# Third block of a hybrid decoder trunk: head outputs with tokens on partitions, and where the norm factor is applied

## The reference

```python
def _head_norm(o, g, center):
    if center:
        o = o - jnp.mean(o, axis=-1, keepdims=True)
    o = o * lax.rsqrt(jnp.mean(jnp.square(o), axis=-1, keepdims=True) + EPS)
    return o.reshape(o.shape[0], o.shape[1], -1) * g.astype(jnp.float32)

def _mixer_c(h, hg_s, lower_bound, w_in, hg_gn, w_out):
    qp, fp, ip, gp = _split(jnp.einsum('bld,de->ble', h, w_in), C_SPLITS)
    f = lower_bound + (1.0 - lower_bound) * jax.nn.sigmoid(fp)
    q, k, log_f, v = jax.nn.silu(qp), 1.0 - f, jnp.log(f), ip    # 8 heads of 128
    o, s_new = _hgrn2(q, k, log_f, v, hg_s)                      # output and new state of each head
    o = _head_norm(o, hg_gn, False) * jax.nn.silu(gp)
    return jnp.einsum('ble,ed->bld', o, w_out), s_new
```

## Time and profile before

| what | value |
|---|---|
| median of 3 runs | 1494.74 us (1494.48 to 1496.93) |
| the profiled execution | 1494.81 us |
| its span, first to last instruction | 1493.0 us |
| PE busy | 1471.3 us, 99% of the span |
| DVE busy | 1121.7 us, 75% |
| ACT busy | 911.0 us, 61% |
| POOL busy | 89.7 us, 6% |
| mean granted TensorE clock | 0.997 |

### The profile page before, as it was taken

How to read it: one execution, slowest core, us unless ns; L and a number is a source line. 1 busy time by engine, 2 the same in 40 slices (tenths; PEclk the granted TensorE clock), 3 DMA queues, 4 the chain that set the end, 5 groups by cost and what they waited for, 6 DMA issues and landing times.

```text
span 1493.0 us, 22862 instructions
## 1 busy us (share of the span) xinstructions
PE 1471.3 (99%) x8445; PEld 1305.0 (87%) x8445; DVE 1121.7 (75%) x1223; ACT 911.0 (61%) x950; POOL 89.7 (6%) x96
## 2 busy tenths in 40 slices
PE   9999999999999999999999999999999999999997
PEld 8899899999999999998788888888888888888885
DVE  5766678554555587456898888988889888898987
ACT  5434545334333563333777878778787787877875
POOL 1023110000000001210300000000000000000011
PEclk9999999999999999999999999999999999999999
DMA  9577725997455533541999999999999999999994
GB/s 253 133 132 140 147 75 154 284 294 214 116 154 157 181 118 110 147 147 45 402 408 389 394 353 401 378 383 391 358 397 376 385 388 367 393 374 384 399 333 171
DMA packets 213586, 404.02 MB, mean 271 GB/s; under 512 B 13471, under 2 KB 130491, under 8 KB 213390
## 3 DMA queue, kind: packets, MB, share of 16 engines
q1 hardware_dynamic: 202976, 372.82, 71.8%
q0 software_dynamic: 6320, 22.20, 5.1%
q10 hardware_dynamic: 4222, 8.06, 1.4%
HBM read 372.75 MB, written 30.28 MB: 270 GB/s over the span
## 4 chain that ended last, share of the span: by engine, by line
PE 92%; DVE 5%; ACT 1%; issue 1%; POOL 0%; ACTq 0%; DVEq 0%; POOLq 0%
PE bank L523 27%; PE bank L524 27%; PE bank L525 27%; PE bank L752 2%; PE bank L1188 1%; PE bank L1012 1%; DVE dense_lo L1917 1%; PE bank L797 1%; PE bank L697 1%; DVE arena L2057 1%; PE bank L744 1%; PE bank L673 0%; PE bank L1115 0%; DVE w_lo L2396 0%; PE bank L705 0%
## 5 line engine op out<-in xcount | busy, mean ns | idle before, releaser
L2396 DVE TENSOR_TENSOR w_lo<-arena,w_hi 128x2048 fp32r<-128x2048 f32 (+1 forms) x280 | 597.3, 2167 | 82.0 <-ACT w_hi L1755 81.0
L1755 ACT ACTIVATE w_hi<-arena 128x2048 fp32r<-128x2048 f32 (+1 forms) x280 | 502.2, 1820 | 118.7 <-PE bank L525 112.6
L523 PE MATMUL bank<-w_hi,xg_hi 128*128 128x512 f32 x704 | 275.6, 392 | 1.3 <-DVE xg_lo L2454 0.6
L525 PE MATMUL bank<-w_hi,xg_lo 128*128 128x512 f32 x704 | 274.1, 389 | 0.0
L524 PE MATMUL bank<-w_lo,xg_hi 128*128 128x512 f32 x704 | 274.0, 389 | 0.0
L1917 DVE TENSOR_TENSOR dense_lo<-ring,dense_hi 128x2048 fp32r<-128x2048 f32 (+1 forms) x77 | 165.6, 2150 | 120.9 <-ACT dense_hi L1413 120.8
L1413 ACT ACTIVATE dense_hi<-ring 128x2048 fp32r<-128x2048 f32 (+1 forms) x78 | 140.5, 1802 | 136.1 <-PE bank L525 114.5
L523 PEld LDWEIGHTS bank<-w_hi,xg_hi 128*128 128x128 f32 x704 | 132.2, 188 | 31.8 <-issue 3.1
L525 PEld LDWEIGHTS bank<-w_hi,xg_lo 128*128 128x128 f32 x704 | 132.1, 188 | 27.7
L524 PEld LDWEIGHTS bank<-w_lo,xg_hi 128*128 128x128 f32 x704 | 132.2, 188 | 26.8
L523 PE MATMUL bank<-h_hi,dense_hi 128*128 128x320 f32 x448 | 142.9, 319 | 1.3 <-DVE h_lo_a L1987 1.1
(11 more groups left out here) (443 smaller groups left out, 2316.0 us busy)
## 6 DMA issues: line engine op xcount, KB each, us to landing
arena<-in_w_moe_down SPq DMA_DIRECT2D x176, 512.0 KB, 6.8
arena<-in_w_moe_gate SPq DMA_DIRECT2D x128, 512.0 KB, 7.3
arena<-in_w_moe_up SPq DMA_DIRECT2D x128, 512.0 KB, 7.4
arena<-in_w_moe_gate SPq DMA_DIRECT2D x64, 384.0 KB, 4.4
arena<-in_w_moe_up SPq DMA_DIRECT2D x64, 384.0 KB, 5.5
ring<-in_w_in_ab SPq DMA_DIRECT2D x32, 512.0 KB, 8.8
ring<-in_w_in_c SPq DMA_DIRECT2D x32, 512.0 KB, 4.7
expert_rows<-ZERO SPq DMA_DIRECT2D x12, 1024.0 KB, 7.8
```

The lines of the kernel that those rows point to most:

```text
L523: mm(out, left[0], right[0], start=start, stop=False)
L525: return mm(out, left[1], right[0], start=False, stop=stop)
L1755: fn(WH[SLOT_OF[p]][:, 0:unit_size(p)], STAGE[:, s, 0:unit_size(p)], ACT.Copy).then_inc(S("unit_hi"), 1)
L2396: v.tensor_tensor(WL[w][:, 0:n], STAGE[:, s, 0:n], WH[w][:, 0:n].bitcast(F32), ALU.subtract).then_inc(S("unit_split"), 1)
```

## The change

The head's output is made with tokens on partitions: PH's blocks are the weights and the values V are the moving operand. For the sample tokens, the weights are the head's 64 sample queries, each sequence's 8 placed in columns of its own in an otherwise zero 64-column buffer (QB, two buffers), and the 128-column state is the moving operand. POOL fills QB at the start of each turn step: it sets both buffers to zero once, and per head copies 128 x 64 numbers to the places. ACT copies the rows out into PH's place and squares them with a running sum per token (three instructions with accum_out). ACT's root and DVE's reciprocal then work on a number per token and head, DVE multiplies the rows by it (three blocks in one instruction), and PE transposes each head back, three transposes per head. The gate step multiplies gain and gate straight from that PSUM bank. The products for mean squares and for spreading factors are gone. In C_STEPS the sq and varc steps are gone, gates follow their head's transposes, and rootc1 stands ahead of state7.

The diff, cut to its core:

```diff
-    v1 ub0 mb0 lb0 v2 wh ub1 mb1 lb1 wl turn0 v3 ub2 mb2 lb2 out0 v4 sq0 ub3 mb3 lb3 state0 turn1 v5 wh ub4 mb4 lb4 wl out1 v6 sq1 ub5 mb5 lb5 state1 turn2 v7 ub6 lb6
-    out2 v8 wh sq2 ub7 lb7 state2 turn3 wl v9 lb8 kend1 part1 out3 v10 sq3 state3 v11 wh turn4 wl g0 out4 g1 wh sq4 wl state4
-    turn5 g2 out5 g3 wh sq5 wl state5 silug0 varc0 rootc0 turn6 g4 gate0 gate1 out6 g5 wh sq6 wl gate2 gate3 state6
-    turn7 mixc0 mixc1 g6 mixc2 mixc3 out7 h0 h1 g7 h2 h3 sq7 silug1 silug2 gate4 gate5 state7 gate6 gate7 wh mixc4 mixc5 wl
-    h4 h5 varc1 rootc1 mixc6 mixc7 h6 h7
+    v1 ub0 mb0 lb0 v2 wh ub1 mb1 lb1 wl turn0 v3 ub2 mb2 lb2 out0 v4 ub3 mb3 lb3 state0 turn1 v5 wh ub4 mb4 lb4 wl out1 v6 ub5 mb5 lb5 state1 turn2 v7 ub6 lb6
+    out2 v8 wh ub7 lb7 state2 turn3 wl v9 lb8 kend1 part1 out3 v10 state3 v11 wh turn4 wl g0 out4 g1 wh wl state4
+    turn5 g2 out5 g3 wh wl state5 silug0 rootc0 turn6 g4 out6 g5 wh wl state6 turn7 mixc0 gate0 mixc1 gate1 g6 mixc2
+    gate2 mixc3 gate3 out7 h0 h1 g7 h2 h3 silug1 silug2 rootc1 state7 mixc4 gate4 mixc5 gate5 wh wl h4 h5 mixc6 gate6
+    mixc7 gate7 h6 h7
...
-        SQH = {"hn0": [region(NT * u, NT) for u in range(KD)],
-               "hn1": [region(5120 + NT * u, NT) for u in range(KD)]}
+        SQH = {"hn0": [region(NT * u, NT) for u in range(KD)]}
+        ROWS_OF = [PH[:, u, 0:3 * P].rearrange("p (i n) -> p i n", n=P) for u in range(HG)]
+        QB = region(6400, 2, NB, SMP)
...
+            def rows_back(u):
+
+                pe.wait_ge(S("rows_scaled"), u + 1)
+                kind = "dve" if u in HEADS[0] else "act"
+                b = open_bank(kind)
+                for i, (t0, tn) in enumerate(BLK):
+                    ins = nc.tensor.transpose(b[:, t0:t0 + tn], ROWS_OF[u][0:tn, i, :], ident[0:tn, 0:tn])
+                close_bank(kind, ins, ("hn1", "scale", u))
+
-                    if tag == "hn0":
-                        after_empty(pe, ("cen", u))
-                    else:
-                        pe.wait_ge(S("hn1_squares"), u + 1)
+                    after_empty(pe, ("cen", u))
...
-                close_bank(kind, ins, name)
+                close_bank("dve", ins, name)
-            def outputs(layer, u, probs, probs_ready, right):
+            def outputs(u, probs, probs_ready, right):
-                if layer == 0:
-                    pe.wait_ge(S("qe0"), u + 1)
-                else:
-                    pe.wait_ge(S(f"level_up{u // 4}"), 8)
-                pe.wait_ge(S(f"state_in_{layer}_{u % NST}"), 16 * (u // NST + 1))
-                kind = "act" if layer else "dve"
-                b = open_bank(kind)
-                yield from weigh(b, values, probs, right, ST[:, u % NST], ("num", layer, u), kind)
-                if layer == 0 and u >= H4:
+                pe.wait_ge(S("qe0"), u + 1)
+                pe.wait_ge(S(f"state_in_0_{u % NST}"), 16 * (u // NST + 1))
+                b = open_bank("dve")
+                yield from weigh(b, values, probs, right, ST[:, u % NST], ("num", 0, u))
+                if u >= H4:
+
+            def output_rows(u):
+
+                values = lambda i: V[:, i, u * DH:(u + 1) * DH]
+                p = PH[:, u, :]
+                pe.wait_ge(S("chunks_parted"), u // 4 + 1)
+                pe.wait_ge(S(f"state_in_1_{u % NST}"), 16 * (u // NST + 1))
+                pe.wait_ge(S("queries_spread"), u + 1)
+                b = open_bank("act")
+                mm(b[:, 0:P], p[:, 0:P], values(0), start=True, stop=True)
+                mm(b[:, P:TP], p[:, P:TP], values(0), start=True, stop=False)
+                mm(b[:, P:TP], p[:, TP:384], values(1), start=False, stop=True)
+                mm(b[0:SMP, TP:384], p[:, 384:448], values(2), start=True, stop=False)
+                for s in range(NB):
+                    ins = mm(b[0:SMP, TP:384], QB[:, u % 2, s, :], ST[:, u % NST, s, :], start=False, stop=(s == NB - 1))
+                close_bank("act", ins, ("num", 1, u))
...
-                    piece_along(outputs(1, u, PH[:, u, :], lambda: pe.wait_ge(S("chunks_parted"), u // 4 + 1), Q[:, u, TP:NT]))
+                    output_rows(u)
...
-                    free(fn(OH[:, u, :], take(("num", 1, u))[:, 0:NT], ACT.Copy))
-                elif name == "sq":
-                    after_empty(act, ("num", 1, u))
-                    fn(SQH["hn1"][u], OH[:, u, :], ACT.Square).then_inc(S("hn1_squares"), 1)
+                    b = take(("num", 1, u))
+                    fn(ROWS_OF[u][:, 0:2, :], b[:, 0:TP].rearrange("p (i n) -> p i n", n=P), ACT.Copy)
+                    fn(ROWS_OF[u][0:SMP, 2, :], b[0:SMP, TP:384], ACT.Copy)
+                    spent = (Q[:, u, 0:P], Q[:, u, P:TP], K[:, u, 0:P])
+                    for i, (t0, tn) in enumerate(BLK):
+                        ins = fn(spent[i][0:tn], b[0:tn, i * P:(i + 1) * P], ACT.Square, accum_out=SSH[0:tn, u, i:i + 1])
+                    free(ins)
-                    head_roots("hn1", u)
+                    at = slice(HEADS[u][0], HEADS[u][-1] + 1)
+                    after_empty(act, ("num", 1, at.stop - 1))
+                    fn(SSH[:, at, :], SSH[:, at, :], ACT.Sqrt, scale=1.0 / DH, bias=C("eps")).then_inc(S("hn1_roots"), 1)
-                    after_fill(act, ("hn1", "var", 0 if u in HEADS[0] else 1))
...
-                    head_reciprocals("hn1", u)
-                elif name == "mixc":
-                    dve.wait_ge(S("gated1"), u + 1)
-                    scaled_head(OH, "hn1", u)
+                    at = slice(HEADS[u][0], HEADS[u][-1] + 1)
+                    dve.wait_ge(S("hn1_roots"), u + 1)
+                    step(v.reciprocal(SSH[:, at, :], SSH[:, at, :]))
+                    for h in HEADS[u]:
+                        v.tensor_tensor(ROWS_OF[h], ROWS_OF[h], SSH[:, h, :].unsqueeze(2).to_broadcast([P, 3, P]),
+                                        ALU.mult).then_inc(S("rows_scaled"), 1)
-                    dve.wait_ge(S("hn1_squares"), u + 1)
-                    v.scalar_tensor_tensor(out=OH[:, u, :], in0=OH[:, u, :], scalar=prow("hg_gn", u), in1=GC[:, u, :],
-                                           op0=ALU.mult, op1=ALU.mult).then_inc(S("gated1"), 1)
+                    b = take(("hn1", "scale", u))
+                    free(v.scalar_tensor_tensor(out=OH[:, u, :], in0=b[:, 0:NT], scalar=prow("hg_gn", u), in1=GC[:, u, :],
+                                                op0=ALU.mult, op1=ALU.mult))
...
             after_fill(pool, ("fd", KD - 1))
-            g.memset(V[SMP:P, 2, :], 0.0)
+            g.memset(V[SMP:P, 2, :], 0.0).then_inc(S("queries_zero"), 1)
             for u in range(NST):
                 if name == "turn":
+                    if u == 0:
+                        pool.wait_ge(S("level_up1"), 2)
+                        pool.wait_ge(S("queries_zero"), 1)
+                        g.memset(QB[:, :, :, :], 0.0).then_inc(S("queries_zero"), 1)
+                        pool.wait_ge(S("queries_zero"), 2)
+                    if u >= 1:
+                        pool.wait_ge(S("vx1"), u)
+                    if u >= 2:
+                        after_fill(pool, ("num", 1, u - 2))
+                    pool.wait_ge(S("hgrn_kend"), u // 4 + 1)
+                    w = QB[:, u % 2, 0:1, 0:1]
+                    own = bass.AP(tensor=w.tensor, offset=w.offset, ap=[list(w.ap[0]), [SMP + TS, NB], [1, TS]])
+                    g.tensor_copy(own, Q[:, u, TP:NT].rearrange("p (s t) -> p s t", t=TS)).then_inc(S("queries_spread"), 1)
+                    pool.wait_ge(S("queries_spread"), u + 1)
                     if u % 2 == 0:
                     spread(1, u)
```

More of the change, by code:

```diff
@@ L325, in trunk_kernel @@
         NS0 = small[:, 24:56]
+        SSH = small[:, 432:432 + 3 * HG].rearrange("p (h i) -> p h i", i=3)
         NRAW = small[:, 56:92].rearrange("p (h n) -> p h n", n=9)
@@ L740, in turn_keys, with weigh @@
                 close_bank("act", ins, ("kn", layer, u))
-            def weigh(b, left, probs, right, states, name, kind="dve"):
+            def weigh(b, left, probs, right, states, name):
                 mm(b[:, 0:TP], left(0), probs[:, 0:TP], start=True, stop=False, skip_group_check=True)
@@ L894, in _ @@
                 elif name == "weigh":
-                    piece_along(outputs(0, u, PB[:, u % 2, :], lambda: after_empty(pe, ("sc", 0, u)), QE[:, u % 2, :]))
+                    piece_along(outputs(u, PB[:, u % 2, :], lambda: after_empty(pe, ("sc", 0, u)), QE[:, u % 2, :]))
                 elif name == "state":
@@ L929, in projection_out @@
                         for u in HEADS[1]:
-                            head_scale(heads, u)
+                            rows_back(u)
                     if kind == "oab" and k == AB_HIGH[-1]:
@@ L1037, in _ @@
                         tile_done()
-                elif name == "varc":
-                    head_variances("hn1", u)
                 elif name == "mixc" and u in HEADS[0]:
-                    head_scale("hn1", u)
+                    rows_back(u)
```

(1 more changed line is left out.)

## The result

The changed kernel took 1510.7 us (median of 5, 1509.1 to 1521.5), the kernel before 1494.5 us on the same chip; the ratio is 1.0113, with a 95% interval of 1.0093 to 1.0134. The forecast was 1498.8 us with a range up to 1502.0: right in sign, 12 us short.

What follows compares the result with a forecast made beforehand. PE was taken to bound the kernel: +2.9 us until head 7's output (-4.6 PE work, +7.9 POOL waits, -0.45 ACT) and +1.15 in the tail gave +4.0, so 1498.8 us, range 1493.5 to 1502.

Steps and rivals of the forecast that it cites:

- mean squares and factors gone: PE's removed products in the third block: mean squares 3.36 and 1.19 us, spreading factors 5.0 us.
- transposes, 8 heads: PE's three added transposes for each head, 0.27 us a head, 2.2 us in all, bounds 1.6 to 4.4.
- outputs, 8 heads: PE's twelve output products per head at 0.22 us each: 2.64 us against 2.58, 0.05 more a head.
- wait of head 0: PE waits 0.3 us for head 0's queries, behind QB's clearing, POOL's copy and VX.
- waits of heads 1, 2: PE waits for POOL's copy behind the previous head's store: 0.7 us at head 1, 0.15 at head 2.
- wait of head 5: PE waits 2.65 us at head 5's output for POOL's copy, which stands behind head 4's store.
- wait of head 6: PE comes earlier without 3.36 us of mean squares and waits 2.7 us for POOL's copy.
- wait of head 7: PE waits 1.4 us at head 7's output for QB, ready at 666.0.
- silence ahead of the projection: PE idles 4.1 us in the tail until head 7's states free the bank that the projection's second tile wants.
- clock, in the block: Rival: PE's clock falls in the new gaps, time 1499.2 to 1503.3 us, chance 0.2; the forecast sum had none.
- the contention rule: GpSimd contends with DVE instructions with two SBUF inputs; head 6's copy would meet row multiplications, sum staying within bound.
- The rival on the other side: POOL's copy is in time, so none of the 7.9 us of waits arise: 1490.9 us, chance 0.12.

Runs made afterwards that it cites:

- second profile: The changed kernel run and profiled once more with no edit: 1511.8 us, ratio 1.0121.
- tail order: Against the changed kernel, the root and row multiplications of heads 6 and 7 stand behind head 7's states: 1508.4 us, ratio 1.0094.
- VX first: Against the changed kernel, POOL makes VX ahead of the copy of queries for head 0: 1511.8 us, ratio 1.0111.
- the queries ahead: Against the changed kernel, POOL spreads the queries of head u+1 in turn u, behind VX: 1500.75 us, ratio 1.0042.
- the full-row run: Against the changed kernel, each head's third transpose takes all 128 rows instead of 64: 1511.9 us, ratio 1.0121.
- The version that brings this about by construction: Against the changed kernel, queries spread one head ahead and both QB buffers in unused tables, cleared and first filled early: 1494.87 us, ratio 1.0006.

## Why the prediction was 12 us short

The time lay far above the stated range. By its own steps, with the changed kernel's two profiles (the clock is the second's):

| step | forecast, us | measured, us |
|---|---|---|
| mean squares and factors gone | -9.5 | -9.5 (none left) |
| transposes, 8 heads | +2.2 | +4.4 (0.55 a head) |
| outputs, 8 heads | +0.4 | +2.3 (2.87 against 2.58) |
| wait of head 0 | 0.3 | 3.3 |
| waits of heads 1, 2 | 0.85 | 0.8 |
| wait of head 5 | 2.65 | 2.6 |
| wait of head 6 | 2.7 | 3.0 |
| wait of head 7 | 1.4 | 0.4 |
| silence ahead of the projection | 4.1 | 3.3 |
| clock, in the block | 0 (rival, chance 0.2) | 6.8 (8.0 in the first) |

The waits came about as described: POOL's queue order, DVE ahead of the stores, the bank that ties the projection to head 7's states. The projection started 12.65 us after head 7's output, 12.5 was the forecast. Three steps failed, and the first alone is over half of the miss.

**The clock.** The sum had nothing for it. The prediction called this rival "the likelier case" by the Trainium skill's rule, and still gave it 0.2, with the remark that the trace of the kernel before has no idle of such length. That was no evidence against it. It also read the page's clock row as full level in all 40 slices; but a slice is 37 us, and the changed kernel's second profile, with six stretches at 0.50, prints the same 40 nines. In the two profiles of the changed kernel the clock fell at all four long waits, also at those of 2.6 and 3.0 us, which were called less likely. Of the six profiles that kept head 5's wait of 2.6 us unfilled, two (tail order, VX first) don't have it there. Two experiments price it: 6.2 to 7.5 us by filling the waits, and with the queries ahead 11.0 us went, of which 6.8 were waits. The Trainium skill, "TensorE: Matmul & The Clock Gate", section "HAM oscillation — how this bites in real kernels", says that waits between groups of matmuls bring the lower clock back each time; the trace agrees for the waits of 3.0 us and more, and in four of six profiles for that of 2.6.

**POOL's copy for head 0.** The prediction took 0.3 us, with 1.05 as the upper bound, and used the contention rule only for head 6. The copy took 4.2 us, because it meets DVE's row of two-operand instructions, and PE's wait was 3.3. The row that should have set the bound is DVE's own timeline at that place. The trace of the kernel before had a sign of it: VX of head 3, beside DVE's weight split, took 1.88 us where others take 1.05.

```profile
609.49 1.88 POOL L2623 TENSOR_TENSOR arena<-arena,cst 64x512 f32<-64x512 f32 x1
```

The length of DVE's row alone doesn't give the price, though. In the changed kernel, head 1's copy starts beside another such row (L2300), and head 6's copy and VX stand inside six row multiplications without a gap (L2397); none of them is held to the end:

```profile
600.17 0.40 POOL L2713 COPY arena<-arena 128x64 f32<-128x64 f32 x1
...
671.65 0.62 POOL L2713 COPY arena<-arena 128x64 f32<-128x64 f32 x1
672.36 1.23 POOL L2648 TENSOR_TENSOR arena<-arena,cst 64x512 f32<-64x512 f32 x1
...
670.65 3.83 DVE L2397 TENSOR_TENSOR arena<-arena,small 128x384 f32<-128x384 f32 x6
```

Why the row at head 0 holds POOL throughout and these don't was not taken apart. Undone, with the low clock behind it, head 0's wait is worth 5.9 us.

**PE's small products.** 2.2 us too little for the transposes and 1.9 for the outputs. The third transpose's 64-row weights were not loaded ahead (0.25 us each, shown by the full-row run). Why the outputs take 0.29 us more was not taken apart: four products of 128 columns in 1.03 us against 0.82 for the three before, and 1.84 against 1.76 for the states.

The sum of the measured column is 17.4 us. About 2 us of it were covered by waits of the kernel before that fell away, which leaves 15.4; the second profile shows 16.0 between the first turn and the router's roots. Behind that point the two profiles are 0.6 and 1.7 us longer than the kernel before. In that stretch, the router, the clock was low for a time in all but three of the twelve profiles with the change and not in the profile before; it falls around a wait of PE for ACT of 0.9 to 1.0 us, which the kernel before has as well. That this comes from the change is not shown.

The rival on the other side, that POOL's copy comes in time, was priced at 1490.9 us. The version that brings this about by construction took 1494.9, 4.0 us more: the products cost 4.1 us more than forecast, and the clock still fell in the tail.

## What to carry to other kernels

When a change gives PE a new thing to wait for, find the queue of the engine that makes it and what stands ahead there. If it is a store that waits for a third engine, move the new step a turn earlier rather than make it quicker. Price a silence of PE like those here (2.6 to 3.3 us) as the silence plus 1.7 us of slow clock, at times 3, and look whether removing PE work only brings PE to the next wait sooner.

## What the runs showed of the hardware

- At PE's silences of 2.6 to 3.3 us (heads 0, 5, 6, projection) the granted clock went to 0.50, from inside the silence to 1.6 us behind its end. It did so in every profile where they were not filled, but for head 5's 2.6 us, where it did in four of six. Each fall cost 1.5 to 1.7 us of work, the long ones 2.2 to 3.0. A wait of 2.2 us at head 4 was followed by it in one profile of two. Waits of up to 1.1 us in the same block were not.
- Silence is not the only sign to look for. In the router the clock fell around a wait of 0.9 to 1.0 us in nine of twelve profiles; in the kernel before it fell at 208 us with no wait above 0.35 us ahead of it. In three executions with the change it also fell in the first layer, between 99 and 131 us, for 1.7 to 8.5 us of lost work, where nothing was edited. The cause of these is open.
- A POOL instruction that starts beside DVE instructions with two SBUF operands can be held until their row ends: 4.2 us for a copy that takes 0.25 us alone, 4.9 for a VX of 1.0. Beside other such rows the same copy took 0.40 and 0.62 us.
- Filling waits with products that nobody reads made the kernel 7.5 us faster (6.2 to 7.5 in the block).
- A transpose with 64-row weights among 128-row ones cost 0.25 us more than a full one.
